# Three quarters of a sum over all experts on TensorE, the last 512 columns gathered per pick and added by VectorE

## What is computed

```python
def peer_ffn(h, w_pq, peer_keys, peer_u, peer_v):
    ...
    idx = jnp.take_along_axis(cidx, pos, axis=-1)          # 16384 = 128 x 128 experts
    gate = jax.nn.softmax(top_s, axis=-1).astype(h.dtype)
    def one_block(args):
        x_blk, i_blk, g_blk = args
        u = jnp.take(peer_u, i_blk, axis=0)
        a = jax.nn.gelu(jnp.einsum("td,thkd->thk", x_blk, u)) * g_blk
        v = jnp.take(peer_v, i_blk, axis=0)
        return jnp.einsum("thk,thkd->td", a, v)
```

## Time and profile before

| | us |
|---|---|
| median of 3 runs | 3504.51 |
| lowest and highest | 3502.84, 3505.26 |
| profiled execution, its time | 3506.31 |
| profiled execution, its span | 3504.5 |

### The profile page before, as it was taken

The page is one execution under the profiler, slowest core; times in us unless marked ns, Lnnn a source line. Parts: engine busy times, 40 slices in busy tenths (PEclk is TensorE's granted clock), DMA queues, the critical chain, the costliest instruction groups (busy, mean ns, idle before and its releaser), DMA issues. The chain is left out here.

```text
span 3504.5 us, 37031 instructions
## 1 busy us (share of the span) xinstructions
PE 2712.1 (77%) x12521; PEld 2253.7 (64%) x12521; DVE 2313.0 (66%) x3294; ACT 1445.4 (41%) x2311; POOL 565.8 (16%) x308
## 2 busy tenths in 40 slices
PE   6796999999999979998899950001420599999998
PEld 5665778888888868687787950001320488888886
DVE  3698555545455554544655589999999995555555
ACT  4333244343434454344344420003950584444444
POOL 0200001010101000000100037777677100000000
PEclk9898599999999989899999985555555799999999
DMA  7452155555555535154455659999999775666664
GB/s 223 139 164 80 58 183 180 193 191 192 183 190 189 192 108 180 54 198 162 169 193 177 206 213 420 391 389 394 393 392 393 309 276 216 225 222 254 219 216 167
DMA packets 244035, 779.40 MB, mean 222 GB/s; under 512 B 28889, under 2 KB 36289, under 8 KB 189024
## 3 DMA queue, kind: packets, MB, share of 16 engines
q1 hardware_dynamic: 206832, 509.53, 43.0%
q0 software_dynamic: 36864, 268.45, 19.2%
q10 hardware_dynamic: 240, 0.18, 0.0%
HBM read 773.92 MB, written 4.19 MB: 222 GB/s over the span
## 5 line engine op out<-in xcount | busy, mean ns | idle before, releaser
L194 DVE TENSOR_TENSOR wl<-ring,wh 128x1024 fp32r<-128x1024 f32 (+2 forms) x680 | 823.7, 1252 | 652.3 <-ACT wh L189 649.9
L189 ACT CAST wh<-ring 128x1024 fp32r<-128x1024 f32 (+2 forms) x680 | 673.9, 1041 | 768.8 <-PE ps L210 690.4
L208 PE MATMUL ps<-wh,th 128*128 128x512 f32 (+1 forms) x1632 | 639.7, 392 | 42.2 <-DVE wl L194 34.6
L209 PE MATMUL ps<-wl,th 128*128 128x512 f32 (+1 forms) x1632 | 634.6, 389 | 0.0
L210 PE MATMUL ps<-wh,tl 128*128 128x512 f32 (+1 forms) x1632 | 634.3, 389 | 0.0
L1977 DVE CUSTOM_DVE_ANT_0 junk<-expert_rows,h 128x2048 f32<-128x2048 f32 x256 | 570.2, 2287 | 10.3 <-DMA expert_rows<-in_peer_u,index 9.5
L1587 POOL DMA_INDIRECT expert_rows<-in_peer_u,index x256 | 482.5, 1885 | 572.6 <-PE ps L1673 385.9
L2007 DVE TENSOR_TENSOR wl<-ring,wh 128x1024 fp32r<-128x1024 f32 x256 | 302.1, 1221 | 267.9 <-ACT wh L2198 267.0
L2198 ACT CAST wh<-ring 128x1024 fp32r<-128x1024 f32 x256 | 256.8, 1053 | 315.7 <-PE ps L2075 314.3
L208 PEld LDWEIGHTS ps<-wh,th 128*128 128x128 f32 x1632 | 308.3, 189 | 115.5 <-DVE wl L194 44.5
L210 PEld LDWEIGHTS ps<-wh,tl 128*128 128x128 f32 x1632 | 308.1, 189 | 63.4
(11 more groups left out here) (329 smaller groups left out, 3327.2 us busy)
## 6 DMA issues: line engine op xcount, KB each, us to landing
ring<-in_peer_v SPq DMA_DIRECT2D x160, 1024.0 KB, 5.3
ring<-in_w_in SPq DMA_DIRECT2D x112, 1024.0 KB, 5.0
ring<-in_w_up SPq DMA_DIRECT2D x64, 1024.0 KB, 5.3
ring<-in_w_down SPq DMA_DIRECT2D x64, 1024.0 KB, 5.1
ring<-in_w_out SPq DMA_DIRECT2D x32, 1024.0 KB, 5.2
ring<-in_w_peer_q SPq DMA_DIRECT2D x16, 1024.0 KB, 5.4
ring<-in_w_ukv SPq DMA_DIRECT2D x8, 1024.0 KB, 5.2
ring<-in_w_uq SPq DMA_DIRECT2D x8, 768.0 KB, 4.5
```

The lines of the kernel that those rows point to most:

```text
L189: self.nc.scalar.copy(self.wh[:, i % 2, two, 0:w], self.ring[:, i, two, 0:w]).then_inc(self.high_ready, 1)
L194: self.nc.vector.tensor_tensor(self.wl[:, i % 2, two, 0:w], self.ring[:, i, two, 0:w], self.wh[:, i % 2, two, 0:w].bitcast(F32), ALU.subtr ...
L208: mm(o, hi, wh, start=start and k == 0, stop=False)
L209: mm(o, hi, wl, start=False, stop=False)
```

## The change

The early rounds and the sum over all experts are made for the first V_TILES = 3 column tiles only (1536 columns), so a slab is 6 KB per partition where it was 8, and a slab's two parts are 1024 and 512 columns. The slab buffers move to a place that the dots' row buffers left. For the last 512 columns GpSimd gathers, for each pick n, the last quarter of the picked row of `peer_v` (128 pieces of 2 KB), into one of 8 buffers `expert_pieces`, and VectorE multiplies it with the token's weight and adds it to `pieces_summed`. Two adds stand behind each slab of the main loop's VectorE code, eight a group; in the first group the eight stand behind the third and fourth slab. The piece's index is 4 x expert + 3, made by VectorE in the dots stage (`index_pieces`). Gather n waits for the add of pick n - 8. At the end VectorE adds the sums of pieces to x before the banks.

```diff
+V_TILES = 3
+    v_pieces = peer_v.rearrange("e (c n) -> (e c) n", c=4)
+    parts_of = (slice(0, 2), slice(2, V_TILES))
+        slabs = place("expert_slabs", [P, RING, V_TILES, 512], at=-112 * KB)
+        sh = place("expert_slab_high", [P, 2, V_TILES, 512], F32R, at=-88 * KB)
+        sl = place("expert_slab_low", [P, 2, V_TILES, 512], F32R, at=-76 * KB)
+        pieces = place("expert_pieces", [P, GR, 512], at=-64 * KB)
+        summed = place("pieces_summed", [P, NH, 512], at=88 * KB)
...
+            for m in range(PRE):
+                if m < RING:
+                    sp.wait_ge(freed, NH * PICKS + (m * V_TILES + V_TILES - 1) // 4 + 1)
+                else:
+                    sp.wait_ge(core.low_ready, base * (2 * RING) + 2 * (m - RING) + 2)
+                sp.dma_start(slabs[:, m % RING], only(m)).then_inc(core.landed[m % RING], 16)
...
+            pool.wait_ge(freed, NH * PICKS + GR)
+            pool.wait_ge(pieces_indexed, NH)
+            for n in range(UNITS * TOPK):
+                if n >= GR:
+                    pool.wait_ge(piece_used, n - GR + 2)
+                nc.gpsimd.indirect_dma_start(
+                    pieces[:, n % GR, :], None, v_pieces,
+                    bass.IndirectOffsetOnAxis(ap=piece_at[n // PICKS][:, n % PICKS:n % PICKS + 1], axis=0)
+                ).then_inc(piece_landed[n % GR], 16)
...
+            def index_pieces():
+                step.all(*[nc.vector.scalar_tensor_tensor(out=piece_f[half], in0=p.keys_of[:, 0, half_of(half)], scalar=float(NKEYS),
+                                                          in1=p.keys_of[:, 1, half_of(half)], op0=ALU.mult, op1=ALU.add)
+                           for half in range(NH)])
+                for half in range(NH):
+                    nc.vector.tensor_scalar(piece_at[half], piece_f[half], 4.0, float(V_TILES), ALU.mult, ALU.add).then_inc(
+                        pieces_indexed, 1)
...
-                for part in range(2):
-                    two = slice(2 * part, 2 * part + 2)
+                for part, two in enumerate(parts_of):
                     dve.wait_ge(half_high, g * 2 * RING + (2 * i + part + 1))
-                    nc.vector.tensor_tensor(core.wl[:, i % 2, two], core.ring[:, i, two], core.wh[:, i % 2, two].bitcast(F32),
+                    nc.vector.tensor_tensor(sl[:, i % 2, two], slabs[:, i, two], sh[:, i % 2, two].bitcast(F32),
                                             ALU.subtract).then_inc(half_low, 1)
+            def add_piece(g, half, j):
+                dve.wait_ge(piece_landed[j], g * 16 + 16)
+                dve.wait_ge(piece_used, g * GR + (j + 1))
+                nc.vector.scalar_tensor_tensor(out=summed[:, half, :], in0=pieces[:, j, :],
+                                               scalar=weight[:, bass.ds(g * GR + j, 1)], in1=summed[:, half, :],
+                                               op0=ALU.mult, op1=ALU.add).then_inc(piece_used, 1)
+            def group_low(g, half):
                 for i in range(RING):
                     main_low(g, i)
+                    for j in range(2 * i, 2 * i + 2):
+                        add_piece(g, half, j)
+            for i in range(RING):
+                main_low(0, i)
+                if i == 1:
+                    dve.wait_ge(core.slabs_used, main * RING + 2)
+                    nc.vector.memset(summed[:], 0.0).then_inc(piece_used, 1)
+                if i >= 2:
+                    for j in range(4 * i - 8, 4 * i - 4):
+                        add_piece(0, 0, j)
+            for half in range(NH):
+                with dve.Fori(1 if half == 0 else groups // 2, (half + 1) * groups // 2) as g:
+                    group_low(g, half)
...
+            dve.wait_ge(piece_used, UNITS * TOPK + 1)
+            for half in range(NH):
+                c = slice(V_TILES * 512, D)
+                nc.vector.tensor_tensor(x[:, half, c], summed[:, half, :], x[:, half, c], ALU.add).then_inc(added, 1)
             for half in range(NH):
                 dve.wait_ge(core.slabs_used, (main + groups) * RING + 1 + half)
-                for q in range(4):
+                for q in range(V_TILES):
...
-                for part in range(2):
+                for part, two in enumerate(parts_of):
                     pe.wait_ge(half_low, g * 2 * RING + (2 * i + part + 1))
                     for half in range(NH) if i < RING - 1 else (1,):
...
-                            for k in (2 * part, 2 * part + 1):
+                            for k in range(two.start, two.stop):
```

More of the change, by code:

```diff
@@ L1845, in peer_stage, with full, only @@
     v_rows = peer_v.rearrange("(a g i) (c n) -> i a g c n", a=NKEYS, i=RING, c=4)
+    v_pieces = peer_v.rearrange("e (c n) -> (e c) n", c=4)
     main = base + PRE // RING
[L1848 to L1852, removed]
+    parts_of = (slice(0, 2), slice(2, V_TILES))
+    def full(g, i):
+        return v_rows[i, :, bass.ds(g, 1), 0:V_TILES, :].rearrange("a g c n -> a (g c) n")
+    def only(m):
+        return v_rows[RING - 1, :, m, 0:V_TILES, :]
     with ExitStack() as local:
@@ L1863, in peer_stage @@
         half_high, half_low = core.new("half_slabs_high", "half_slabs_low")
+        piece_used, pieces_indexed = core.new("pieces_used", "pieces_indexed")
+        piece_landed = core.new(*[f"piece_landed{i}" for i in range(GR)])
         landed, rows = p.landed, p.rows
@@ L1898, in load_group @@
                     sp.wait_ge(half_low, g * 2 * RING + (2 * i + 2 - 2 * RING))
-                    sp.dma_start(core.ring[:, i], full(g)(i)).then_inc(core.landed[i], 16)
+                    sp.dma_start(slabs[:, i], full(g, i)).then_inc(core.landed[i], 16)
             for i in range(RING):
-                core.load_slab(sp, full(0), main, i)
+                sp.wait_ge(core.low_ready, base * (2 * RING) + 2 * (PRE - RING + i) + 2)
+                sp.dma_start(slabs[:, i], full(0, i)).then_inc(core.landed[i], 16)
             with sp.Fori(1, groups // 2) as g:
@@ L1963, in early_low @@
                                         eh[:, m % 2, :].bitcast(F32), ALU.subtract).then_inc(w_low, 1)
-                core.split_low(dve, base + m // RING, m % RING)
+                for part, two in enumerate(parts_of):
+                    dve.wait_ge(core.high_ready, base * (2 * RING) + (2 * m + part + 1))
+                    nc.vector.tensor_tensor(sl[:, m % 2, two], slabs[:, m % RING, two], sh[:, m % 2, two].bitcast(F32),
+                                            ALU.subtract).then_inc(core.low_ready, 1)
+            def index_pieces():
[5 more added lines that the diff above has]
+                        pieces_indexed, 1)
             nc.vector.memset(core.small[:, 60:61], 0.0).then_inc(freed, GR)
@@ L1988, in _ @@
                         weigh(0)
+                    if n == PICK_DOTS + 4:
+                        index_pieces()
             weigh(1)
@@ L2022, in _ @@
                 mine = slice(half, half + 1)
-                dve.wait_ge(sums, 4 * half + 4)
+                dve.wait_ge(sums, NH + (half + 1) * V_TILES)
                 final_step(nc.vector.tensor_reduce(ms[:, mine], sums_of[:, 4 * half:4 * half + 4], AX.X, ALU.add))
@@ L2058, in early_slab @@
                 pe.wait_ge(core.low_ready, base * (2 * RING) + 2 * m + 2)
-                wh, wl = core.wh[:, m % 2], core.wl[:, m % 2]
+                wh, wl = sh[:, m % 2], sl[:, m % 2]
                 for n, (weights, v) in enumerate(((eh, wh), (eh, wl), (el, wh))):
-                    for k in range(4):
+                    for k in range(V_TILES):
                         end = mm(core.ps[:, k, :], weights[:, m % 2, :], v[:, k, :], start=m == 0 and n == 0, stop=False)
@@ L2066, in slab @@
                 pe.wait_ge(w_low, g * RING + (PRE + i + 1))
-                wh, wl = core.wh[:, i % 2], core.wl[:, i % 2]
-                for part in range(2):
+                wh, wl = sh[:, i % 2], sl[:, i % 2]
+                for part, two in enumerate(parts_of):
                     pe.wait_ge(half_low, g * 2 * RING + (2 * i + part + 1))
@@ L2145, in early_high @@
                 nc.scalar.copy(eh[:, m % 2, :], by_expert[:, 0, RING * m + RING - 1, :]).then_inc(w_high, 1)
-                core.split_high(act, base + m // RING, m % RING)
+                act.wait_ge(core.landed[m % RING], (base + m // RING) * 16 + 16)
+                act.wait_ge(core.slabs_used, base * RING + (m + 1))
+                for two in parts_of:
+                    nc.scalar.copy(sh[:, m % 2, two], slabs[:, m % RING, two]).then_inc(core.high_ready, 1)
             exponentiate(0)
@@ L2195, in main_high @@
                 act.wait_ge(core.slabs_used, (g + main) * RING + (i + 1))
-                for part in range(2):
-                    two = slice(2 * part, 2 * part + 2)
-                    nc.scalar.copy(core.wh[:, i % 2, two], core.ring[:, i, two]).then_inc(half_high, 1)
+                for two in parts_of:
+                    nc.scalar.copy(sh[:, i % 2, two], slabs[:, i, two]).then_inc(half_high, 1)
```

(7 more changed lines are left out.)

9 lines of the change are left out of this document (2 added, 7 removed).

## The result

The changed kernel takes 3366.7 us (median of 4 runs, 3365.9 to 3367.2) against 3504.9 before: a ratio of 0.961, 95% interval 0.959 to 0.962. The forecast of 3354 had the sign and the mechanism; the gain is 138 us where 151 were expected. The profiled execution has a span of 3365.3 us.

What follows compares the result with a forecast made beforehand. TensorE bounds the sum over all experts. 3504.5 - 152.5 (fewer matmuls) + 12.8 (short-slab gap) + 2.1 + 1 - 16.5 (early rounds) + 1.1 + 1.0 = 3353.5, so 3354 us; range 3336 to 3410.

Steps and rivals of the forecast that it cites:

- TensorE's floor: Main loop: 63 matmuls a group instead of 84, 14.29 us a group, 457.4 us in all, a gain of 152.5 us.
- The short slab: Main loop, each group's fourth slab: 2.04 us of matmuls cannot cover a 2.31 us copy-and-subtract path; 0.4 us a group, +12.8 us.
- VectorE in the main loop: With two adds per slab VectorE needs 14.4 us a group, just under the 14.7 us period, about 98% busy.
- GpSimd: Main loop gathers wait for the VectorE instruction they meet: 1.65 us each, 13.2 us a group, hidden under 14.7.
- Rival (2): Main loop gathers keep the dots' pace of 2.21 us: 17.7 us a group, 3449 us in all; chance 10%.
- rival (3): Main loop VectorE instructions wait for running gathers, up to 0.94 us each: 21.9 us a group, 3581 us; chance 3%.
- the band of 13.3 to 14.0 us: Main loop: time a group for the DMA engines to move 5.24 MB, taken from full-queue rates; 15.3 from partial-load packet times.
- Rival (1): Transfers set the main loop's pace: 15.3 us a group gives 3373 us, 16.2 gives 3402; chance 23%.
- rival (4): Main loop slowed by landing latency of the eight piece buffers: 20.4 us a group, 3533 us; chance 4%.
- The small terms: First group's adds +2.1 us, reload of x and gains +1, early rounds -16.5, piece indexing in the dots +1.1, tail +1.0.
- The clock: Main loop: TensorE's gaps might lower its granted clock; at 0.95 this would add 5% of 457 us; not in the sum.
- Early rounds: Sixteen rounds before the main loop: VectorE sets 6.55 us a round, a gain of about 16.5 us, bounds 10 to 22.

Runs made afterwards that it cites:

- both edits: Changed kernel with the slab's 512-column part first and the reload of x and gains issued in three pieces; 3341.3 us, 0.953 of the kernel before.
- the last experiment: The kernel before the change, its first four early slab loads issued only when all dots are done; 3503.2 us in one run, beside 3505.2.
- the transfers alone: Changed kernel with the 512-column part first, adds replaced by one-column memsets, third matmul product left out of the main loop, all loads and gathers kept; 3314.1 us.

## Why the prediction was right, and where it was off

**TensorE's floor** held: 63 matmuls in 14.28 us once nothing else is in the way.

**The short slab** was the right mechanism, and the term was mis-sized: 0.4 us a group forecast, 0.65 measured (14.94 less 14.29), 8 us in all. The step took 2.31 us of path against 2.04 of matmuls. The path is 0.02 + 1.06 + 0.03 + 1.24 + 0.04 = 2.39 in the chain above; and the 54 matmuls on the chain last 12.55 us, not the 12.25 of 54 intervals. Of the 0.30 between, some 0.16 is there because a chain that leaves TensorE must wait for the end of the last matmul, where the next matmul need only wait for its start. The other 0.13 lies in the first matmuls behind the gap: the first two take 0.57 us to the third and not 0.45 (2926.20 to 2926.77). Of the forecast's 0.4, the part for "two semaphores" stood for all that and was too small.

**VectorE in the main loop** came out at the forecast 14.4 us, 14.40 when it is the bound, and in part by luck, since two terms in it were off and cancelled. That two adds would be within 0.3 us of TensorE's pace, and would cost nothing as long as the gap is open, held as well. VectorE's timeline of the changed kernel shows one full slab:

```profile
3112.05 0.42 DVE L2038 TENSOR_TENSOR weights_low_part<-by_expert,weights_high_part 128x256 fp32r<-128x256 f32 x1
3112.39 1.82 DVE L2042 TENSOR_TENSOR expert_slab_low<-expert_slabs,expert_slab_high 128x1024 fp32r<-128x1024 f32 x2
3114.12 1.64 DVE L2048 SCALAR_TENSOR_TENSOR pieces_summed<-expert_pieces,const,pieces_summed 128x512 f32<-128x512 f32 x2
3115.68 0.42 DVE L2038 TENSOR_TENSOR weights_low_part<-by_expert,weights_high_part 128x256 fp32r<-128x256 f32 x1
```

The pair of adds takes 1.56 us and not 1.45, the first step 0.34 and not 0.44; the sum is 3.63 for 3.64. Its share was 94% and not 98, since the period is 14.94.

**GpSimd** was right: 1.65 us a gather forecast, 1352 ns and 0.30 measured. Rival (2), the dots' pace of 2.21, did not come. The gather's side of the wait was confirmed by taking the adds away; VectorE's side was not there: between 2900 and 3060 us its adds take 749 ns beside the gathers and 748 without, and it is busy for 149.8 us and 149.7. So rival (3) is refuted here: 8 gathers a group took nothing from VectorE. By the rule of the Trainium skill's page "SBUF — State Buffer", section "Who interferes with whom", whoever issues first holds the shared pair and the other blocks; for a VectorE instruction with two SBUF inputs the page says so beside a GpSimd instruction that reads SBUF. The trace agrees on the gather's side alone, and no run here shows for how long a gather holds the pair, if at all.

**DMA**: the band of 13.3 to 14.0 us held (13.4 to 13.7). Rival (1) stayed a rival, 1.2 us a group away, and rival (4) too: with the small part first, pieces land in 7.7 us and slabs in 7.4 in the median, against 11 and 11.7 of slack.

**The small terms** were put 8.3 us too low at the reload and the start. The reload was put at +1 us, since 8 us of delay stood against 7 of slack; it cost 6.1. Of these 4.5 are the late slab. The delay was about right: 16.29 us to landing, where slabs land in 7.3 to 7.4 beside gathers (medians of two of the edited kernels), are 8.9. The slack was not: 11.7 less 7.4 is 4.3, and 7 is near what is left with the 4.5 us of a load that has the DMA engines to itself. Without the gathers, where slabs land in 4.6, the slabs behind the reload land in at most 10.3 us and nothing is lost. The start was put at +2.1 and cost 5.3: the first group's 2.4, from the adds as forecast, and 2.9 in the second.

**The clock** was named under "wrong, too" and stands in no term of the sum. It took 4.5 us, 2.9 in the second group and 1.6 behind the reload. The gaps of 0.65 us in every group did not lower it (1.00 in both stages); what came before the two falls was 2.75 us of idle time and, at the reload, 4.9. In what way idle time lowers the clock stays open: 2.68 us left it at 1.00 without the gathers, and 2.07 us was followed by 0.51 with both edits but by 1.00 with the small part first alone.

Early rounds (-16.0 for -16.5) and the tail (+1.1 for +1.0) held. The end of the dots came 3.3 us early where indexing was to put it 1.1 late: a term that wasn't seen, gathers and slab loads in one another's way, which the last experiment showed in the kernel before.

The early end of the dots is luck: without it the miss of 12 us would have been 16. Of the signs, the gathers of 1.35 us and the slices of 350 GB/s came as told; one chain piece of 2016 matmuls did not come, and by the forecast's own gap could not. In the working, 14.7 - 1.8 - 1.1 is 11.8 and not 11.7, and the times of rivals (3) and (4) leave out the 3.1 us of small terms that those of (1) and (2) keep; neither changes anything.

Together: 8.0 (gap) + 5.1 (reload) + 3.2 (start), less 4.4 (dots) and 0.6 (the last group has no gap), plus 0.5 + 0.1 (early rounds, tail) are the 12 us between forecast and span. The clock's 4.5 are in the terms of reload and start.

## What to carry to other kernels

When work is cut from the engine that is the bound, look for the shortest stretch that it used to cover: here a path of 2.4 us over two other engines was hidden by 2.72 us of matmuls and bare over 2.04, and the smaller part of the slab first shortened it so that it was hidden again, which was worth 17 us. Three resources at 94 to 98% busy didn't say which one set the pace; leaving out the adds and the gathers, one at a time, did: both were free in the steady loop. Large one-off transfers belong in pieces no larger than the buffers' slack, in a queue that also feeds a tight loop; that slack is reckoned with the landing times of the loaded loop, not of a load alone. Where a group takes longer than the others, look at the granted clock before looking for a late transfer.

## What was not expected of the hardware

A DMA busy share of 97% was no bound: 349 GB/s at 97% in the changed kernel, 384 to 391 GB/s at 100% when the transfers were alone, with packets of 2 and 6 KB mixed.

A gather on GpSimd costs 0.98 us when VectorE's adds are gone and 1.35 with them, while VectorE's adds cost the same with and without gathers (748 and 749 ns): the wait goes one way.

With TensorE busy 134 of 160 us the granted clock was 0.89 to 0.91 of the full 2.4 GHz; with 156 of 160 it was 1.00. Single idle times of TensorE between 2 and 6.4 us in the main loop (the transfers alone left aside) were followed by a clock of 0.50 for 3 to 6 us in eight places, but by 1.00 in two (2.07 us with the small part first, 2.68 us without the gathers).
